# Which side of the array the gates' products load: x or the 64 weight columns

## The reference, cut to what matters

```python
h = x @ w_in[l]
dq, dk, dv, dz, db, da, aq, ak, av, ga, gb = jnp.split(h, split_at, axis=-1)
...
beta = jax.nn.sigmoid(beta_logit.astype(jnp.float32))
g = -jnp.exp(a_log) * jax.nn.softplus(a_logit.astype(jnp.float32) + dt_bias)
```

## Time and profile before

| | |
|---|---|
| Median of 3 runs | 1897.86 us (1897.86 to 1898.42) |
| The profiled execution | 1897.5 us, its span 1895.6 us |
| TensorE busy | 1882.3 us, 9703 products and 9703 loads |
| VectorE, ScalarE, GpSimd busy | 1314.4, 918.2 and 209.6 us |
| Mean granted TensorE clock | 0.998 |
| HBM traffic | 204 GB/s over the span |

### The profile page before, as it was taken

The page is one execution under the profiler, slowest core; times in us unless marked ns, Lnnn a source line. Parts: engine busy times, 40 slices in busy tenths (PEclk is TensorE's granted clock), DMA queues, the critical chain, the costliest instruction groups (busy, mean ns, idle before and its releaser), DMA issues.

```text
span 1895.6 us, 30058 instructions
## 1 busy us (share of the span) xinstructions
PE 1882.3 (99%) x9703; PEld 1555.3 (82%) x9703; DVE 1314.4 (69%) x1832; ACT 918.2 (48%) x1270; POOL 209.6 (11%) x480
## 2 busy tenths in 40 slices
PE   9999999999999999999999999999999999999997
PEld 7888888878888888888888887888888888888886
DVE  7878788787666767675577657677764566655656
ACT  5655565654454545456444447444443444443442
POOL 0303031131023232323000000000000000000000
PEclk9999999999999999999999999999999999999999
DMA  7666666574557676766666674555655555555555
GB/s 282 204 195 215 202 201 222 175 237 155 195 194 245 211 246 217 245 216 211 198 198 197 224 244 167 200 190 196 195 194 192 196 190 196 192 195 194 189 192 174
DMA packets 115091, 387.62 MB, mean 204 GB/s; under 512 B 14192, under 2 KB 21168, under 8 KB 114864
## 3 DMA queue, kind: packets, MB, share of 16 engines
q1 hardware_dynamic: 97904, 351.65, 55.9%
q10 hardware_dynamic: 11712, 22.04, 3.5%
q0 software_dynamic: 5376, 12.59, 2.4%
HBM read 367.86 MB, written 18.37 MB: 204 GB/s over the span
## 4 chain that ended last, share of the span: by engine, by line
PE 97%; DVE 1%; DMA 0%; issue 0%; ACT 0%; SPq 0%; DVEq 0%; ACTq 0%
PE pg L486 92%; PE B L486 5%; DVE gates L1463 1%; DMA raw<-in_weights 0%; PE B L586 0%; PE B L605 0%; PE B L699 0%; ACT whi L866 0%; PE B L812 0%; DVE wlo L1455 0%; DVE act_b L1455 0%; PE B L740 0%; DVE lnst L2135 0%; DVE sm L1463 0%; DVE lnst L2140 0%
## 5 line engine op out<-in xcount | busy, mean ns | idle before, releaser
L1455 DVE TENSOR_TENSOR wlo<-raw,whi 128x1024 fp32r<-128x1024 f32 (+1 forms) x640 | 778.7, 1219 | 476.7 <-ACT whi L866 457.7
L866 ACT ACTIVATE whi<-raw 128x1024 fp32r<-128x1024 f32 (+1 forms) x640 | 673.5, 1057 | 740.0 <-PE pg L486 720.8
L486 PE MATMUL pg<-whi,act_x 128*128 128x512 f32 x2960 | 937.2, 393 | 0.5 <-ACT whi L866 0.5
L486 PEld LDWEIGHTS pg<-whi,act_x 128*128 128x128 f32 x2960 | 556.1, 188 | 119.2 <-issue 2.7
L486 PE MATMUL pg<-wlo,act_x 128*128 128x512 f32 x1480 | 574.6, 390 | 0.0
L486 PE MATMUL pg<-whi,act_a 128*128 128x512 f32 x1632 | 504.7, 389 | 0.1
L486 PEld LDWEIGHTS pg<-whi,act_a 128*128 128x128 f32 x1632 | 306.4, 188 | 64.1 <-DVE act_a L1455 0.8
L486 PEld LDWEIGHTS pg<-wlo,act_x 128*128 128x128 f32 x1480 | 278.1, 188 | 54.7
L486 PE MATMUL pg<-wlo,act_a 128*128 128x512 f32 x816 | 317.4, 389 | 0.0
L486 PEld LDWEIGHTS pg<-wlo,act_a 128*128 128x128 f32 x816 | 153.2, 188 | 31.7
L486 PE MATMUL pg<-whi,act_b 128*128 128x512 f32 x512 | 158.4, 389 | 0.0
(11 more groups left out here) (259 smaller groups left out, 1098.7 us busy)
## 6 DMA issues: line engine op xcount, KB each, us to landing
raw<-in_weights SPq DMA_DIRECT2D x646, 512.0 KB, 3.9
turn_c<-hraw ACTq DMA_DIRECT2D x8, 512.0 KB, 4.0
qT<-turn_c POOLq DMA_DIRECT2D x32, 128.0 KB, 3.1
turn_q<-hraw ACTq DMA_DIRECT2D x6, 512.0 KB, 3.9
gates<-turn_q ACTq DMA_DIRECT2D x24, 128.0 KB, 4.3
turn_p<-gates POOLq DMA_DIRECT2D x12, 192.0 KB, 3.5
gates<-turn_p POOLq DMA_DIRECT2D x48, 48.0 KB, 3.9
decm<-sums_out ACTq DMA_DIRECT2D x4, 512.0 KB, 3.7
```

Of the source, the lines that this page charges most:

```text
L486: return nc.tensor.matmul(o, l, r, start=start, stop=stop)
L866: return nc.scalar.activation(o, i, ACT.Copy, scale=scale)
L1455: return V.tensor_tensor(o, a, b, op)
```

## The change

The 64 weight columns and x change sides. In slots 3 and 4 there are now 64 products (16 chunks, 2 token blocks, 2 parts of x), each with 128x128 of x loaded and 64 weight columns moving; token block t is summed in `B[t]`, with tokens on partitions. So the turn in slot 5 goes, with ScalarE's copy, VectorE's matrix of identities and three semaphores (`pe_abT`, `act_abT`, `dve_two`). What the turn also did, to add the high and the low columns, VectorE does: for each token block a copy of the low half out of PSUM into `ab` (a view of `oh`) and an addition of the high half, four operations of 128x32, chained. `dt` is then added from `ab`, and ScalarE's exponential for beta reads `ab`. TensorE's wait for the constants moves from slot 5 to slot 8.

```diff
--- before.py
+++ after.py
@@ -245,6 +245,7 @@
         xres = [b[:, :, :].rearrange("p h s -> p (h s)").rearrange("p (t n) -> p t n", t=TOK) for b in (qT, kT)]
         w_first = flat(AT[:, :, :])[:, 0:NG].rearrange("p (k c) -> p k c", c=2 * HEADS)
         w_ab2 = act_a[:, 0, 0:4, :].rearrange("p a b -> p (a b)").rearrange("p (k c) -> p k c", c=4 * HEADS)
+        ab = oh[:, :, 0:2 * HEADS]
         warm = flat(TTf[:, :, :])
         centre, sums = (flat(QKT[:, :, :])[:, i * P:(i + 1) * P] for i in range(2))
         vtok = flat(kT[:, :, :]).rearrange("p (a q x) -> p a q x", a=4, x=SB)
@@ -340,7 +341,7 @@
         out_full = sem("out_full")
         x_hi = sem("x_hi")
         x_lo = sem("x_lo")
-        once = """pe_passed pe_ab pe_abT act_ab2 dve_ab2 act_abT dve_two pe_sc0 act_pro dve_pro dve_sc0 act_tot dve_lam act_lam
+        once = """pe_passed pe_ab act_ab2 dve_ab2 pe_sc0 act_pro dve_pro dve_sc0 act_tot dve_lam act_lam
             dve_lnT dve_x1 pe_x1T x1f act_x1T dve_x1T pe_y act_beta act_gc pe_gT act_gT act_var dve_var act_root act_sig act_xn pro_chain ln_chain""".split()
 
         counted = """pe_conv dve_raw dve_conv act_silu dve_cw act_tap
@@ -542,19 +543,14 @@
                         if k in (8, 12):
                             pe.wait_ge(x_hi, k // 4 + 2)
                             pe.wait_ge(x_lo, k // 4 + 2)
-                        for f in range(2):
-                            last = mm(B[0][0:4 * HEADS, 0:SEQ], w_ab2[:, k, :], act_x[:, f, k, :],
-                                      k == f == 0, k == KC - 1 and f == 1)
+                        for t in range(TOK):
+                            for f in range(2):
+                                last = mm(B[t][:, 0:4 * HEADS], act_x[:, f, k, t * P:(t + 1) * P], w_ab2[:, k, :],
+                                          k == f == 0, k == KC - 1 and f == 1)
                     if s == 4:
                         last.then_inc(N["pe_ab"], 1)
-                if s == 5:
+                if s == 8:
                     pe.wait_ge(const_full, 48)
-                    pe.wait_ge(N["act_abT"], 1)
-                    pe.wait_ge(N["dve_two"], 1)
-                    for t in range(TOK):
-                        last = mm(B[1][:, 32 * t:32 * t + 32], oh[0:4 * HEADS, t, :], pz[0:4 * HEADS, 3, :])
-                    last.then_inc(N["pe_abT"], 1)
-                if s == 8:
                     pe.wait_ge(N["dve_pro"], 1)
                     mm(B[3][:, 0:32], c("same"), g_all[:, :])
                     mm(B[3][:, 32:64], c("after"), g_all[:, :])
@@ -906,9 +902,6 @@
                     act.wait_ge(ab_full, 16)
                     copy(w_ab2[:, :, 0:2 * HEADS], w_first).then_inc(N["act_ab2"], 1)
                 if s == 5:
-                    act.wait_ge(N["pe_ab"], 1)
-                    copy(oh[0:4 * HEADS, :, :], B[0][0:4 * HEADS, 0:SEQ].rearrange("p (t d) -> p t d", t=TOK)
-                         ).then_inc(N["act_abT"], 1)
                     act.wait_ge(const_full, 48)
                     act.wait_ge(N["dve_sc0"], 1)
                     nc.scalar.activation(pz[:, 1, :], pz[:, 1, :], ACT.Exp, scale=-1.0)
@@ -916,7 +909,7 @@
                                          ).then_inc(N["act_pro"], 1)
                     for t in range(TOK):
                         last = nc.scalar.activation(scal[:, :, 4 * t:4 * t + 4],
-                                                    B[1][:, 32 * t:32 * t + HEADS].rearrange("p (j h) -> p j h", h=HB),
+                                                    ab[:, t, 0:HEADS].rearrange("p (j h) -> p j h", h=HB),
                                                     ACT.Exp, scale=-1.0)
                     last.then_inc(N["act_beta"], 1)
                     act.wait_ge(N["dve_lam"], 1)
@@ -1513,8 +1506,6 @@
                        ).then_inc(N["dve_ab2"], 1)
                 if s == 4:
                     dve.wait_ge(const_full, 48)
-                    tt(pz[0:4 * HEADS, 3, :], ident[0:4 * HEADS, 0:2 * HEADS], ident[0:4 * HEADS, 2 * HEADS:4 * HEADS],
-                       ALU.add).then_inc(N["dve_two"], 1)
                 if s == 11:
                     m0, e0, i0 = (CONST[n][0] for n in ("pairs", "eye", "incl"))
                     levels = cst[:, m0:m0 + 6 * CH].rearrange("p (m c) -> p m c", c=CH)
@@ -1537,9 +1528,12 @@
                                     ).then_inc(N["dve_lam"], 1)
                 if s == 5:
                     dve.wait_ge(const_full, 48)
-                    dve.wait_ge(N["pe_abT"], 1)
-                    for t in range(TOK):
-                        pro(tt(pz[:, 0, t * HEADS:(t + 1) * HEADS], B[1][:, 32 * t + HEADS:32 * t + 2 * HEADS], par[:, slice(*PARAM["dt"])],
+                    dve.wait_ge(N["pe_ab"], 1)
+                    for t in range(TOK):
+                        pro(V.tensor_copy(ab[:, t, :], B[t][:, 2 * HEADS:4 * HEADS]))
+                        pro(tt(ab[:, t, :], ab[:, t, :], B[t][:, 0:2 * HEADS], ALU.add))
+                    for t in range(TOK):
+                        pro(tt(pz[:, 0, t * HEADS:(t + 1) * HEADS], ab[:, t, HEADS:2 * HEADS], par[:, slice(*PARAM["dt"])],
                                ALU.add))
                     stt(pz[:, 1, :], pz[:, 0, :], -1.0, pz[:, 0, :], ALU.mult, ALU.max).then_inc(N["dve_sc0"], 1)
                     dve.wait_ge(N["act_pro"], 1)
```

## The result

Eight executions of each gave a median of 1903.09 us after (1900.76 to 1904.71) and 1898.08 us before (1897.86 to 1900.82). The ratio of the two is 1.0024, with a 95% interval from 1.0016 to 1.0033: slower by 0.24%, 4.6 us by that ratio (the two medians lie 5.0 us apart), where 2.3 us was forecast. The profiled execution of the changed kernel has a span of 1900.8 us, 5.2 us over that of the kernel before, and took 1902.66 us. The executions also spread more than those of the kernel before, over 3.9 us against 3.0 us.

The account below looks back on a forecast made before the run. TensorE was taken to bound the kernel. Adding 6.82 us of products and removing 4.52 us gave +2.3 us on 1897.86 us, so 1900.2 us, with a range from 1898.6 to 1902.8 us.

Parts of the forecast that it names:

- What bounds the kernel: TensorE, busy 1882.3 of 1895.6 us with 97% of the chain; changes to its queue reach the end at full size.
- What is removed: TensorE slots 3, 4 and 5: 32 products and the turn go, 1.93 + 1.82 + 0.77 = 4.52 us.
- The price of a product: Slots 3 and 4: 0.1065 us for each product loading 128 columns and moving 64, taken from slot 14's records.
- The term of 6.82 us: Slots 3 and 4, added on TensorE: 64 products at 0.1065 us; the ends give 6.2 and 7.4 us.
- Rival 3: Slots 3 and 4: loads faster than the plain rate, products 3.5 us, a gain of 1.0 us to 1896.9 us; chance 0.06.
- Rival 1: Slots 3 and 4: load and movement do not overlap, 136 ns a product, +4.2 us to 1902.1 us; chance 0.13.
- rival 2: Granted clock falls after poorly fed slots 3 and 4; at half, tile 4 costs +2.7 us more, 1902.9 us; chance 0.07.
- the argument from the stretch `B<-cT`: Slot 14's 16 records keep the clock at 1.00, cited against a clock fall, though lasting 1.7 us and not 3.4.
- What it does to the others: VectorE in slot 5 does not wait for `pe_ab`; four added operations cost 0.88 us, its chain ending at 34.5 us.
- The cover of 3.7 us: Time between VectorE's gate chain ending at 34.5 us and TensorE needing it in slot 8 at 38.2 us.
- Rival 4: VectorE comes late in slot 8; its chain must grow 3.7 us beyond the 0.9 us worked out; chance 0.02.
- No DMA is added or moved.: DMA adds nothing to the time; the queue bringing the weights waits for the splits and not for TensorE.

Follow-up runs that it names:

- Experiments 3 and 8: Changed kernel with its 64 products regrouped: 3, four runs of 16 in place of two of 32, median 1902.02 us; 8, one run of 64, 1905.97 us.
- experiment 7: Changed kernel with 128 moving columns in each of the 64 products in place of 64; median 1901.26 us.
- experiment 1: The repeat: the changed kernel again without an edit, nine executions beside the kernel before; median 1902.98 us against 1898.44 us.
- experiments 9 to 12: Four runs of 16, and the kernel before plus 22 own-kind products, each with and without the sums' broadcast: 1901.49 and 1900.70 us; 1901.11 and 1900.43 us.

## Why the prediction was right in its direction and short in its size

**What bounds the kernel.** Right. TensorE is 96% of the chain, and its delay at tile 9 stands in the end to the full 4.24 us.

**What is removed.** 4.52 us was taken off; with it the sum at tile 9 closes to 0.01 us.

**The price of a product.** Forecast 0.1065 us, measured 0.109 (3.49 us for 32) in the changed kernel and 0.110 with 128 columns moving. The term of 6.82 us was 6.98 us, and the 0.09 us at the end of the second run was not in it: 2.55 us where 2.3 us stood. The reading of the loads' durations held: 128 columns of x load in 192 ns (median of the 64), as for f32. The Trainium skill ("TensorE: Matmul & The Clock Gate", section "Weight-path perf modes") has a fast weight load on for 128 columns of a type that is not FP32. For fp32r it didn't show here: the loads last 192 ns and the products stand 0.109 us apart. Rival 3 fell with it. Rival 1 fell too: load and movement overlap.

**The clock, rival 2.** Here the forecast failed. The mechanism was named, its place too (tile 4, behind a poorly fed run), and put at 0.07; it came in the profiled execution and by the mean clocks in at least six of nine of the repeat. The step that was wrong is the argument from the stretch `B<-cT`: it took 1.7 us with 128 columns moving, and I let its clock of 1.00 speak for 3.5 us with 64. Experiments 3 and 8 speak for the length and experiment 7 for the columns; the counts of falls in them are least numbers. The price was set too high: a full 2.7 us on tile 4, measured 1.49 us there and 0.29 us ahead, because the clock came back before the tile ended. On the mean the clock is worth some 1.1 us (0.0 to 2.3, experiment 1 less experiment 3, whose own products cost 0.2 us more), so that its size is not well known.

The Trainium skill ("TensorE: Matmul & The Clock Gate", section "HAM oscillation — how this bites in real kernels") lays a falling clock to gaps in which TensorE waits between bursts. In this case there was no such gap: PE is busy 4.01 of 4.01 us in the stretch in which the clock fell.

**What it does to the others.** VectorE was forecast not to wait for `pe_ab`; it did wait, its chain ended later than the 34.5 us of the forecast, and it made no difference. Its timeline:

```profile
29.46 0.19 DVE L1533 COPY oh<-B 128x32 f32<-128x32 f32 x1 [1.02 <-PE B L487]
...
35.15 0.21 DVE L1453 TENSOR_SCALAR lam<-lam 128x1 f32<-128x1 f32 x1
```

It waited 1.02 us for `pe_ab`, since the slow clock and the products pushed that sign to 29.4 us; the chain ended at 35.4 us, and TensorE's slot 8 came at 40.17 us. The cover of 3.7 us that was worked out is 4.8 us. Rival 4 fell.

**"No DMA is added or moved."** True of the program, but not of the time at which they meet. TensorE's delay moves the prologue's sums, and with them their write and their broadcast, and the weight stream is held by TensorE as well, since ScalarE's split waits for a used tile. I had said that the queue waits for the splits and not for TensorE, and took what the change does to TensorE to reach the end at full size and no more; that was the second failed step. Its term: 0.6 to 0.7 us on the mean (experiments 9 to 12, one of the two intervals with zero in it), 0.32 us in the profiled execution (3.93 less 3.61).

The mean difference of 4.8 us in experiment 1 is then 2.55 for the products, 1.1 for the clock and 0.6 to 0.7 for the sums' way through memory: 4.3 us, an estimate from three measurements with wide intervals. The remaining 0.5 us is inside the intervals. The wait of 0.4 us for `Tc` in slot 21 stands in this one profile and in none of the other thirteen; its cause is open.

The chance was put 0.78 on a change within 0.2%. The measured 0.24% lies just beyond it, by the two terms above, though its interval (0.16 to 0.33%) takes in the 0.2%. Of the range, which ended at 1902.8 us, the same can be said: 0.24% on the 1897.86 us of the forecast is 1902.4 us, inside, and the median of 1903.09 us is 0.3 us outside. That the time fell near that end is luck: the end was set there for rival 1, a dearer product, which did not come.

## What to carry to other kernels

When both sides of a small product can be the loaded one, count what each side costs: here a product that loads 64 columns and moves 256 took 0.116 us and one that loads 128 and moves 64 took 0.109, so 32 of the first (3.7 us) were cheaper than 64 of the second (7.0 us), though half as many columns moved and the turn fell away. Price a long run of load-bound products with the clock: break it up, or move more columns, and look at the granted clock in the tile behind it. And when the bounding engine is delayed early (here by 2.5 to 4 us, for 0.6 to 0.7 us more), follow what is tied to it and lands by DMA, not only the engines' queues: its slack was taken for granted because the kernel before showed no wait.

## What the runs showed that I had not expected

- The granted clock fell to half while TensorE was busy without a gap: in a run of 64 products with 128 columns loaded and 64 moving in each of five executions, in two runs of 32 in at least ten of seventeen, in runs of 16 in at least one of 44, and in runs of 32 with 128 columns moving in none of eleven that the mean clock would show.
- Moving 64 or 128 fp32r columns behind a load of 128 costs the same, 0.109 and 0.110 us.
- A plain delay of 2.55 us on the bounding engine, in well-fed products, made the kernel 3.6 us slower (2.9 to 4.2), and 3.0 us (2.4 to 3.6) without the sums' way through memory.
- The mean granted clock of an execution, 0.998, was the same with and without 3.4 us at half clock.
